# A one-layer hybrid encoder step on one core: the norm weights move from the token rows into the projection weights

## The reference

```
def rmsnorm(x, g):
    xf = x.astype(jnp.float32)
    y = xf * lax.rsqrt(jnp.mean(xf * xf, axis=-1, keepdims=True) + EPS)
    return (y * g.astype(jnp.float32)).astype(x.dtype)

xn = rmsnorm(x, norm_g)          # norm_g: 2048 weights, one per column of x
h = xn @ w_in                    # w_in: 2048 x 5648
```

## Time and profile before

| | us |
|---|---|
| median of 3 runs | 1795.19 (1794.94 to 1797.36) |
| the profiled execution | 1795.29 |
| its span (first to last instruction) | 1793.5 |
| PE busy | 1765.4 |
| DVE busy | 781.0 |
| ACT busy | 505.8 |
| POOL busy | 529.4 |

### The profile page before, as it was taken

How to read it: one execution, slowest core, us unless ns; L and a number is a source line. 1 busy time by engine, 2 the same in 40 slices (tenths; PEclk the granted TensorE clock), 3 DMA queues, 4 the chain that set the end, 5 groups by cost and what they waited for, 6 DMA issues and landing times.

```text
span 1793.5 us, 30031 instructions
## 1 busy us (share of the span) xinstructions
PE 1765.4 (98%) x10741; PEld 1638.5 (91%) x10741; DVE 781.0 (44%) x1641; ACT 505.8 (28%) x1155; POOL 529.4 (30%) x486
## 2 busy tenths in 40 slices
PE   5999999999999999999999999999999999999998
PEld 5999999989999999999999999999999888878887
DVE  7754540554545421111556666652222543454333
ACT  6311110134333310000344444330011443333332
POOL 4256420322232242332655555542332000000000
PEclk9999999999999999999999999999999999999999
DMA  7432211343444332212333423344534665765654
GB/s 252 142 92 69 85 48 51 91 112 95 112 111 123 93 101 66 77 57 73 102 96 95 129 87 96 91 125 147 165 103 159 200 230 164 220 207 164 198 165 133
DMA packets 246126, 220.78 MB, mean 123 GB/s; under 512 B 26018, under 2 KB 210676, under 8 KB 244596
## 3 DMA queue, kind: packets, MB, share of 16 engines
q1 hardware_dynamic: 171828, 176.68, 31.6%
q10 hardware_dynamic: 74232, 43.23, 8.9%
HBM read 169.71 MB, written 52.24 MB: 124 GB/s over the span
## 4 chain that ended last, share of the span: by engine, by line
PE 95%; DVE 1%; DMA 1%; ACT 1%; issue 0%; POOL 0%; SPq 0%; ACTq 0%; DVEq 0%; POOLq 0%
PE p L1830 20%; PE p L1832 19%; PE p L1831 19%; PE p L1921 7%; PE p L1923 7%; PE p L1925 7%; PE p L896 2%; PE p L592 1%; PE p L1865 1%; PE p L1864 1%; PE p L1866 1%; PE p L620 1%; PE p L1807 1%; PE p L604 1%; PE p L908 1%; PE p L914 1%
## 5 line engine op out<-in xcount | busy, mean ns | idle before, releaser
L1830 PE MATMUL p<-x_hi,w_lo 128*128 128x384 f32 x2016 | 698.0, 346 | 0.0
L1832 PE MATMUL p<-x_hi,w_hi 128*128 128x384 f32 x2016 | 675.5, 335 | 0.0
L1831 PE MATMUL p<-x_lo,w_hi 128*128 128x384 f32 x2016 | 674.5, 335 | 0.0
L1830 PEld LDWEIGHTS p<-x_hi,w_lo 128*128 128x128 f32 x2016 | 379.0, 188 | 15.6 <-issue 13.5
L548 POOL TENSOR_TENSOR w_hi<-raw,small 128x512 fp32r<-128x512 f32 x164 | 173.5, 1058 | 726.6 <-PE p L1832 710.4
L1831 PEld LDWEIGHTS p<-x_lo,w_hi 128*128 128x128 f32 x2016 | 379.4, 188 | 0.2
L1832 PEld LDWEIGHTS p<-x_hi,w_hi 128*128 128x128 f32 x2016 | 378.6, 188 | 0.0
L2110 DVE TENSOR_TENSOR w_lo<-raw,w_hi 128x512 fp32r<-128x512 f32 x192 | 132.1, 691 | 203.4 <-ACT w_hi L1778 203.4
L552 POOL TENSOR_TENSOR w_lo<-raw,w_hi 128x512 fp32r<-128x512 f32 x164 | 216.2, 1318 | 12.8
L1778 ACT ACTIVATE w_hi<-raw 128x512 fp32r<-128x512 f32 x192 | 121.0, 633 | 238.1 <-PE p L1925 209.7
L1921 PE MATMUL p<-w_hi,x_lo 128*128 128x512 f32 x576 | 162.1, 390 | 1.1 <-DVE w_lo L2110 1.0
(11 more groups left out here) (185 smaller groups left out, 1771.8 us busy)
## 6 DMA issues: line engine op xcount, KB each, us to landing
raw<-in_w_out SPq DMA_DIRECT2D x192, 256.0 KB, 3.4
raw<-in_w_in SPq DMA_DIRECT2D x164, 256.0 KB, 4.3
h_t<-xn SPq DMA_DIRECT2D x126, 192.0 KB, 1.9
work<-h_t SPq DMA_DIRECT2D x24, 384.0 KB, 6.0
out<-work SPq DMA_DIRECT2D x36, 256.0 KB, 4.4
work<-h_t ACTq DMA_DIRECT2D x16, 512.0 KB, 4.6
work<-h_t ACTq DMA_DIRECT2D x32, 256.0 KB, 3.9
work<-in_x_prompt SPq DMA_DIRECT2D x32, 256.0 KB, 5.1
```

The costliest lines, as they stand in the source:

```text
L1830: pe.matmul(out, w_lo[:, k, :], x_hi[:, k, tok], start=(k == 0), stop=False)
L1831: pe.matmul(out, w_hi[:, k, :], x_lo[:, k, tok], start=False, stop=False)
L1832: mm = pe.matmul(out, w_hi[:, k, :], x_hi[:, k, tok], start=False, stop=(k == KT - 1))
```

## The change

The norm weights no longer multiply the token rows. DVE multiplies a tile's rows by the one number per row (a TENSOR_SCALAR instead of a SCALAR_TENSOR_TENSOR with a second input). POOL multiplies each chunk of weights, in place, by the norm weights of its 512 rows, one per partition and k-step, ahead of its split. The weights come as a 16 x 128 tile that PE transposes into PSUM and DVE copies to `g_col`. The 1 MB broadcast load of `g_row` goes; its place in SBUF becomes a fourth buffer for token rows. The constants load moves up to second place, and the first load of item 1's weights no longer waits for tile 7 to be transposed but for tile 5.

```
-        x_buf = [work[:, 0:D_MODEL], raw[:, :], xn[:, :]]
-        g_row = work[:, D_MODEL:2 * D_MODEL]
+        x_buf = [work[:, 0:D_MODEL], raw[:, :], xn[:, :], work[:, D_MODEL:2 * D_MODEL]]
+        g_rows = work[0:KT, 4 * D_MODEL:4 * D_MODEL + P]
...
             load_x(0)
-            sp.dma_start(g_row, norm_g[0:1, :].to_broadcast([P, D_MODEL])).then_inc(s_norm, 16)
+            sp.dma_start(consts_sb[:, :], consts[:, 0:C_MASK0]).then_inc(s_ident, 16)
+            sp.dma_start(g_rows, norm_g.rearrange("a (k p) -> (a k) p", p=P)).then_inc(s_ident, 16)
             load_x(1)
-            sp.dma_start(consts_sb[:, :], consts[:, 0:C_MASK0]).then_inc(s_ident, 16)
             load_x(2)
             for q in range(4):
                 sp.dma_start(w_raw(0, 4 * q, P), w_v[:, 4 * q:4 * q + 4, Q0:Q0 + P]).then_inc(s_w[q], 16)
+            load_x(3)
...
                     if type(j) is int and j == 1:
-                        sp.wait_ge(s_xt, 4 * NTP + 4)
+                        sp.wait_ge(s_xt, 4 * 5 + 8)
...
             for k in ks:
                 pool.wait_ge(s_w[k // 4], 16 * j + 16)
+                pool.tensor_tensor(w_raw(j, k, n), w_raw(j, k, n), g_col[:, k:k + 4].unsqueeze(2)
+                                   .to_broadcast([P, 4, n]), ALU.mult).then_inc(s_wg, 1)
+            for k in ks:
+                pool.wait_ge(s_wg, 4 * j + (k // 4 + 1))
                 pool.wait_ge(s_wfree, 4 * j + (k // 4 + 1))
                 pool.tensor_tensor(w_hi[:, k:k + 4, 0:n], w_raw(j, k, n), zeros[:, :].unsqueeze(1)
                                    .to_broadcast([P, 4, n]), ALU.add).then_inc(s_whi, 1)
...
             pool.wait_ge(v_w[q], 32)
+            pool.tensor_tensor(v_raw[:, ks, :], v_raw[:, ks, :], g_col[:, ks].unsqueeze(2).to_broadcast([P, 4, NV]),
+                               ALU.mult).then_inc(v_whi, 1)
...
+                if t == 1:
+                    pool.wait_ge(s_ident, 34)
                 if 1 <= t < 5:
                     split(pool, 0, ks=(4 * (t - 1),))
...
-            pe.wait_ge(s_ident, 16)
+            pe.wait_ge(s_ident, 32)
+            pe.transpose(ss_bank[:, 0:KT], g_rows, ident[0:KT, 0:KT]).then_inc(s_ident, 1)
...
-            dve.wait_ge(s_norm, 16)
+            dve.wait_ge(s_ident, 33)
+            dve.tensor_copy(g_col[:, :], ss_bank[:, 0:KT]).then_inc(s_ident, 1)
             for t in range(NT):
                 dve.wait_ge(s_rstd, t + 1)
-                dve.scalar_tensor_tensor(out=x_buf[t % 3], in0=x_buf[t % 3], scalar=rstd[:, 0:1],
-                                         in1=g_row, op0=ALU.mult, op1=ALU.mult).then_inc(s_xn, 1)
+                dve.tensor_scalar(x_buf[t % 4], x_buf[t % 4], rstd[:, 0:1], None, ALU.mult).then_inc(s_xn, 1)
```

More of the change, by code:

```diff
@@ L114, in project @@
         small = sb("small", [P, 96])
+        g_col = sb("g_col", [P, KT])
         mhalf, zeros = small[:, 92:93], small[:, 93:94]
@@ L139, in project @@
         ub = banks[3:8]
-        s_norm = sem("s_norm")
         s_ident = sem("s_ident")
         s_const = sem("s_const")
-        s_x = [sem(f"s_x{i}") for i in range(3)]
+        s_x = [sem(f"s_x{i}") for i in range(4)]
         s_w = [sem(f"s_w{i}") for i in range(4)]
@@ L154, in project @@
         s_whi = sem("s_whi")
+        s_wg = sem("s_wg")
         s_wready = sem("s_wready")
@@ L163, in project @@
         s_sqlo = sem("s_sqlo")
-        s_ones = sem("s_ones")
         s_ssq = sem("s_ssq")
@@ L169, in project @@
         s_sig = sem("s_sig")
-        s_zero = sem("s_zero")
+        s_set = sem("s_set")
         s_zst = sem("s_zst")
@@ L356, in _ @@
                 sp.dma_start(gq_col[rows, 1:2], kg.rearrange("a d -> d a")).then_inc(s_const, 16)
-            for t in range(3, NT):
+            for t in range(4, NT):
                 load_x(t)
@@ L483, in _ @@
             sp.dma_start(work[:, 2 * D_MODEL:2 * D_MODEL + M_ALL], tables).then_inc(s_tload, 16)
-            sp.wait_ge(s_zero, 1)
+            sp.wait_ge(s_set, 2)
             for r in range(K0 // P, V0 // P):
@@ L1655, in sum_of_squares @@
             def sum_of_squares(t):
-                act.wait_ge(s_x[t % 3], 16 * (t // 3) + 16)
+                act.wait_ge(s_x[t % 4], 16 * (t // 4) + 16)
                 if t >= 1:
@@ L1660, in sum_of_squares @@
                     act.wait_ge(s_var, t - 1)
-                act.activation(squares, x_buf[t % 3], ACT.Square, accum_out=ss[:, t % 2:t % 2 + 1])\
+                act.activation(squares, x_buf[t % 4], ACT.Square, accum_out=ss[:, t % 2:t % 2 + 1])\
                    .then_inc(s_ss, 1)
@@ L1806, in turn_x @@
                         c = (4 * b + k) * P
-                        mm = pe.transpose(xt_bank[b][:, k * P:k * P + P], x_buf[t % 3][:, c:c + P], ident)
+                        mm = pe.transpose(xt_bank[b][:, k * P:k * P + P], x_buf[t % 4][:, c:c + P], ident)
                     mm.then_inc(s_xt, 1)
@@ L1876, in _ @@
             pe.wait_ge(s_xlo, 4 * NT + 4)
-            pe.wait_ge(s_ones, 1)
+            pe.wait_ge(s_set, 1)
             group(0, NG - 1, stages={(NG - 1) * KT + 2: lambda: sum_squares(0, 0),
@@ L1973, in _ @@
             dve.wait_ge(s_xt, 4 * NT + 4)
-            dve.memset(xn[:, 5 * TN:5 * TN + PAD], 0.0).then_inc(s_zero, 1)
+            dve.memset(xn[:, 5 * TN:5 * TN + PAD], 0.0).then_inc(s_set, 1)
             dve.memset(lr[:, :], 1.0).then_inc(sl_ini, 1)
```

12 lines of the change are left out of this document (6 added, 6 removed).

## The result

The changed kernel took 1820.83 us (median of 4 runs, 1818.19 to 1825.48), the kernel before beside it 1795.67 (4 runs): a ratio of 1.0144, interval 1.0132 to 1.0156. That is slower by 1.4%, as forecast in direction, but 12.8 us above the forecast of 1808.0 and 3.8 us above its range. The profiled execution spans 1819.9 us against 1793.5: 26.4 us to explain. Of all the executions in this document one, of kernel c, ran at a granted clock of 0.75 and took 2391.38 us; c's numbers are without it.

What follows compares the result with a forecast made beforehand. PE was taken to bound the kernel everywhere. From 1795.3 us, minus 3.1 (head), plus 3.8 (item 2), 10 (attention) and 2 (GLA) gave 1808.0 us, slower by 0.7%; the range of 8 in 10 was 1796 to 1817.

Steps and rivals of the forecast that it cites:

- What bounds the kernel: PE sets the time everywhere, practically without a gap from its first product at 31.12 us; any new PE wait loses time.
- The price of a multiplication: Each added POOL multiplication of a weight chunk takes 1.04 us, with 1.3 us as the other bound.
- POOL's total: POOL would be busy about 710 us; the added 183 us or so cost nothing as a sum, given its idle time.
- The hold of DVE by POOL: A DVE instruction waits for a running POOL instruction to end; one, at times two, get in between two of POOL's.
- The head: Before the first product: it starts at 28.0 instead of 31.12 us, 3.1 us gained, bounds 1 to 5.
- Item 2: Four multiplications ahead of the first split delay it 4.15 us; PE waits 3.8 us, bounds 3.3 to 5.
- rival 4: PE's clock falls after waits, 1.6 us each: 1810 if only in item 2, 1821 with seven attention items (chance 0.06).
- The attention items: In seven items multiplications hold DVE's chain before PE's turn: 10 us together, 1.4 an item, bounds 0 to 16.
- The GLA items: Multiplications under DVE's decay levels: 0.2 us of wait times eight, about 1 in the first; 2 us, bounds 0 to 10.
- rival 3: In eight GLA items L1131's third instruction waits for a `w_hi`: 8 us more, 1816 us; chance 0.10.
- The range: The range of 8 in 10 for the whole kernel: 1796 to 1817 us, taking in all of rival 3.
- rival 2: Head gains 5 us, exceeding item 2's wait by 3.6; that wait under 2, no collision: 1792 or less; chance 0.07.

Runs made afterwards that it cites:

- c: Changed kernel with SyncE issuing the loads of item 2's weights before the cache copies; 1817.24 us, ratio 1.0117 to the kernel before.
- d: Changed kernel with each 128x512 multiplication done as four of 128x128 in the same places; 1803.82 us, ratio 1.0044 to the kernel before.
- f: Changed kernel with multiplications for items 11 to 18 begun only after the previous attention item's first two groups' divisions; 1808.72 us, ratio 1.0070 to before.
- g: Changed kernel with multiplications beside the decay levels begun after VectorE's third level, in the decode tile after its second; 1812.22 us, ratio 1.0100 to before.
- b: Kernel before plus multiplications of the weights by ones in the same places from item 1 on, not value columns; 1826.26 us, ratio 1.0174.
- e: Changed kernel with each chunk's multiplication right before its own split instead of all four ahead; 1808.25 us, ratio 1.0074 to the kernel before.
- h: Changed kernel with item 2's weights loaded early, multiplications from item 12 after attention divisions, and those beside decay levels after VectorE's levels; 1793.87 us, ratio 0.9994.
- a: Changed kernel without the multiplications from item 1 on, so those outputs lack the norm weights; 1795.08 us, ratio 0.9997 to the kernel before.

## Why the prediction was right and wrong

- **What bounds the kernel** held. PE has no slack behind its first product, and every new wait of it is in the result; none was given back.
- **The price of a multiplication** (1.04 us) and POOL's total (710 us) held: 1.01 us where nothing held it, 1.09 in the mean, and 712.4 us.
- **The hold of DVE by POOL** held in mechanism. d shows it directly: with pieces of a third of the length (0.37 against 1.02 us) the holds shrink, and POOL's longer busy time does not matter there.
- **The head**: 3.1 us forecast, 2.79 in this execution and 2.0 to 3.5 in others with the same head. That the number is near is in part luck. The first product came at 29.3 instead of 28.0 us, 1.9 us earlier than before and not 3.1; the other 0.9 came from the clock, whose mean from 30 to 32 us was 0.50 in before and 1.00 here. In f, with 0.65 there, the head gave 1.97. The scaling of a tile took 1.28 us where POOL stood still (1.3 in the sum), but 1.61 to 2.03 beside a `w_hi`, which took 1.90 itself.
- **Item 2**: 3.8 forecast, 4.77 measured. The sum and its working disagree here. The working has the weights land no earlier than before, which with PE 3.1 us ahead makes a step of 6.9; the sum takes 3.8, as if they moved along with PE. They did move: issued at 76.13 instead of 78.92, they landed 3.0 us earlier. At full clock the place costs what the sum has, 3.83 us in f. In the changed kernel the wait costs 3.1 us in the ledger (2.93 of them idle), and the matmuls at the lower clock behind it 1.6, under which f's later small waits vanish. That is the first branch of rival 4, which I had priced at 1.6 us and put beside the forecast, not in it. Three kernels that are the same up to there differ: the clock fell in the changed kernel and in g (step 4.80), not in f.
- **The attention items**: 10 forecast, 11.8 measured, in six items of about 2 us and not in seven of 1.4. The estimate of one (1.5 to 2.3 us) was right; I had marked it down by the landing times of the others, mostly without need: only the item with the latest chunks cost nothing, and in c and g it cost 1.5 us too.
- **The GLA items** are the step that failed: "0.2 us of wait, times eight". Measured 7.9 us, 0.9 an item and 1.4 in the first. DVE's four instructions and POOL's four multiplications start where I had them, but I let POOL run at 1.04 us each, as if it held DVE and DVE did not hold it. They hold each other: the multiplications take 4.66 us and the `w_hi` behind them 1.22, and the last L1139 ends beside that `w_hi` at 981.73. Less the 16.28 us that PE was behind there, that is 965.45 instead of 965.0. DVE's slack of 2.4 us was all used up in my sum already, so each tenth more is PE's wait (0.60 us idle), and a wait costs some 0.3 us more than its idle time. This is rival 3, at a chance of 0.10 and 8 us, and its size is right.
- **The decode tile** was missing from the sum: 4.4 us. It runs the same levels after the loop, I counted the items of the loop and stopped there. g shows that it goes by the same cause. The wait costs 2.5 us in the ledger (2.31 idle) and the lower clock behind it 1.8; in b a wait of 2.19 us in the same place was not followed by a fall, and the step was 2.5.
- **The range.** The misses had one sign: 0.3 in the head, 1.0 at item 2, 1.8 in attention, 5.9 in GLA, 4.4 in the decode tile and 0.3 in small steps, 13.7 us against the forecast's span. I had ended the range at the worst of one rival instead of letting several of them come true; they share one cause, so they come together. (The limit of rival 2 was off in itself: its sum, 1792.3, is 3.0 us below before and not 3.6.)

Two things stay open. When the clock falls is not a matter of the wait's length alone: it stayed at 1.00 behind waits of 2.97 us (f, item 2), 2.19 (b, decode tile), 2.13 (c), 2.04 (changed kernel), 1.91 (e, tile 0) and 1.79 (before), and fell behind 2.94 (g, item 2), 2.93, 2.31, 2.02 (c), 1.98 (b) and 1.85 (c, d, f, h). It differs between executions of the same instructions, so a ledger of one execution carries 1 to 2 us of chance at each such wait. And item 2's weights, issued behind the two copies of the caches, landed late: the first chunk came 10.6 to 10.9 us after its issue in before, the changed kernel and a, but 2.9 us after it in c, where it is issued ahead of the copies. So the place behind the copies makes it slow; by what, these runs do not say.

## What to carry to other kernels

Idle time of an engine is not free room: work put on GpSimd costs by what VectorE does in that moment, and by the length of one GpSimd instruction for each VectorE instruction that is held, not by the total. If such work must stand beside a short chain that TensorE waits for, cut it into pieces shorter than the chain's slack, or start it on a semaphore of the chain's end; cut it only where the stream that it is in has time for the fixed cost. When one place of this kind is found in a loop, list every other place with the same instructions, those that run once after the loop too, and let the range carry them all together.

## What the runs showed of the hardware

- A VectorE instruction on 4 elements a partition (0.15 to 0.17 us alone) took up to 1.21 us beside GpSimd instructions of 128x512 and up to 0.41 beside multiplications of 128x128, which last 0.40 us. Several VectorE instructions can pass in between: 0.15 and 0.18 us in the same stretch.
- The hold goes both ways: four GpSimd multiplications took 4.66 us beside VectorE instructions with two inputs and 4.04 alone, and a `w_hi` took 1.90 instead of 1.04 beside a VectorE scaling of 128x2048.
- The same elements multiplied by GpSimd in quarters cost 249.7 us instead of 174.2: 75.5 us over 492 more instructions, 0.15 us for each.
- A fall of TensorE's clock after a wait of 1.85 to 2.93 us cost 1.3 us (h, tile 0) to 1.8 us (decode tile), as much again as half of the wait or more. In c two such falls cost about 3 us in attention.
- Four loads of 256 KB landed in 2.9 to 4.0 us when they were issued ahead of two cache copies on the same queue (c); behind them the first took 10.6 to 10.9 (before, the changed kernel, a).
